# Two unread products around the products by lag, in rounds 3 to 7 of a state space layer on TensorE

## The reference

```python
def s5_mixer(h, w_in, a_re, a_im, log_dt, b_re, b_im, c_re, c_im, d_skip, w_glu, s_re, s_im):
    u = (h @ w_in).astype(f32).reshape(bsz, t, S5_GROUPS, S5_GROUP)
    ...
    bu_re = jnp.einsum('btgi,gpi->btgp', u, bb_re)
    bu_im = jnp.einsum('btgi,gpi->btgp', u, bb_im)
    ...
    _, _, x_re, x_im = lax.associative_scan(combine, (a_re_t, a_im_t, bu_re, bu_im), axis=1)
    y = (jnp.einsum('gip,btgp->btgi', c_re, x_re) - jnp.einsum('gip,btgp->btgi', c_im, x_im)
         + d_skip.astype(f32) * u).reshape(bsz, t, S5_WIDTH)
    za, zg = jnp.split(jax.nn.gelu(y).astype(h.dtype) @ w_glu, 2, axis=-1)
    return za * jax.nn.sigmoid(zg), x_re[:, -1], x_im[:, -1]
```

## Time and profile before

| | us |
|---|---|
| median of 3 runs | 1842.84 |
| lowest and highest run | 1841.28, 1846.24 |
| the profiled execution | 1847.72 |
| its span, first to last instruction | 1845.9 |
| TensorE busy, share of the span | 1734.2, 94% |
| VectorE, ScalarE, GpSimd busy | 1379.5, 1201.8, 146.4 |

### The profile page before, as it was taken

The page is one execution under the profiler, slowest core; times in us unless marked ns, Lnnn a source line. Parts: engine busy times, 40 slices in busy tenths (PEclk is TensorE's granted clock), DMA queues, the critical chain, the costliest instruction groups (busy, mean ns, idle before and its releaser), DMA issues.

```text
span 1845.9 us, 27103 instructions
## 1 busy us (share of the span) xinstructions
PE 1734.2 (94%) x9191; PEld 1457.0 (79%) x9191; DVE 1379.5 (75%) x1579; ACT 1201.8 (65%) x1491; POOL 146.4 (8%) x199
## 2 busy tenths in 40 slices
PE   6988899998899797999999999999999999999994
PEld 3877799986779695887887878878878788788884
DVE  3564445491643736998998989989989899899997
ACT  3623355303463445878888888888888888888885
POOL 1041000000044300700000000000000000000001
PEclk8988999999865698999999999999999999999997
DMA  8662654335630249998998989989989899899995
GB/s 349 257 258 90 237 194 160 141 151 194 289 137 1 103 178 382 399 418 323 422 367 348 410 312 419 392 325 420 360 358 400 314 422 380 343 412 355 399 376 197
DMA packets 72903, 553.49 MB, mean 300 GB/s; under 512 B 8256, under 2 KB 8527, under 8 KB 15328
## 3 DMA queue, kind: packets, MB, share of 16 engines
q1 hardware_dynamic: 69186, 538.54, 73.9%
q0 software_dynamic: 3072, 12.54, 1.8%
q10 hardware_dynamic: 542, 1.20, 0.2%
HBM read 530.74 MB, written 21.53 MB: 299 GB/s over the span
## 4 chain that ended last, share of the span: by engine, by line
PE 84%; DVE 6%; issue 4%; DMA 3%; ACT 2%; POOL 1%; ACTq 0%; DVEq 0%; POOLq 0%; SPq 0%
PE bank L1939 81%; PE bank L2406 1%; DMA ring<-in_dense_rows_dram 1%; DVE w_lo L516 1%; DMA arena<-in_state_conv_dram 1%; DVE arena L1686 1%; ACT w_hi L511 1%; DVE sq L1364 0%; PE bank L2385 0%; DVE rstd L1346 0%; ACT w_hi L463 0%; DVE w_lo L469 0%; DMA fT<-y_rows,row_i 0%; DVE sq L1517 0%; DVE arena L1899 0%
## 5 line engine op out<-in xcount | busy, mean ns | idle before, releaser
L1939 PE MATMUL bank<-w_hi,parts 128*128 128x512 f32 x3024 | 899.0, 392 | 14.8 <-DVE w_lo L516 13.3
L516 DVE TENSOR_TENSOR w_lo<-ring,w_hi 128x1024 fp32r<-128x1024 f32 x654 | 782.4, 1221 | 81.1 <-PE bank L1939 29.8
L511 ACT ACTIVATE w_hi<-ring 128x1024 fp32r<-128x1024 f32 x654 | 690.7, 1062 | 157.4 <-PE bank L1939 157.3
L1939 PEld LDWEIGHTS bank<-w_hi,parts 128*128 128x128 f32 x3024 | 561.6, 188 | 134.1 <-DVE w_lo L516 18.6
L1939 PE MATMUL bank<-w_lo,parts 128*128 128x512 f32 x1512 | 548.3, 390 | 0.0
L1939 PE MATMUL bank<-parts,w_hi 128*128 128x264 f32 x1600 | 312.6, 297 | 21.9 <-DVE parts L1353 21.9
L1939 PEld LDWEIGHTS bank<-w_lo,parts 128*128 128x128 f32 x1512 | 283.9, 188 | 60.3
L1939 PEld LDWEIGHTS bank<-parts,w_hi 128*128 128x128 f32 x1600 | 260.6, 198 | 33.9 <-issue 21.5
L1939 PE MATMUL bank<-parts,w_lo 128*128 128x264 f32 x800 | 234.0, 293 | 0.0
L469 DVE TENSOR_TENSOR w_lo<-ring,w_hi 128x2048 fp32r<-128x2048 f32 x50 | 114.5, 2295 | 148.2 <-ACT w_hi L463 148.2
L1939 PEld LDWEIGHTS bank<-parts,w_lo 128*128 128x128 f32 x800 | 158.0, 198 | 0.0
(11 more groups left out here) (412 smaller groups left out, 1289.4 us busy)
## 6 DMA issues: line engine op xcount, KB each, us to landing
ring<-in_expert_rows_dram SPq DMA_DIRECT2D x330, 1024.0 KB, 7.2
ring<-in_dense_rows_dram SPq DMA_DIRECT2D x48, 2048.0 KB, 8.3
hT<-in_expert_rows_dram SPq DMA_DIRECT2D x55, 1024.0 KB, 7.2
ring<-in_dense_rows_dram SPq DMA_DIRECT2D x8, 1408.0 KB, 6.4
x_rows<-arena SPq DMA_DIRECT2D x1, 7168.0 KB, 28.8
y_rows<-arena SPq DMA_DIRECT2D x10, 512.0 KB, 6.6
arena<-x_rows SPq DMA_DIRECT2D x9, 512.0 KB, 8.1
ring<-in_dense_rows_dram SPq DMA_DIRECT2D x2, 1024.0 KB, 4.8
```

The lines of the kernel that those rows point to most:

```text
L511: act.activation(hi_slots[u % AHEAD], raw_unit(u), ACT.Copy).then_inc(hi_ready, 1)
L516: dve.tensor_tensor(lo_slots[u % AHEAD], raw_unit(u), hi_slots[u % AHEAD].bitcast(F32), ALU.subtract).then_inc(lo_ready, 1)
L1939: return pe.matmul(out, lhsT, rhs, start=start, stop=stop, skip_group_check=True)
```

## The change

The outputs and lag products of a round get a product between them, and the lag products and chunk sums another. It multiplies the identity with the first 256 columns of `xT` and writes bank 0, where nothing reads it. The first stands in rounds 3 to 7, the second in rounds 3 to 6 (round 7 has no lag products): nine in all. Two waits come with it: for the writes of `xT` ahead of the first turns, and for ScalarE's copy of adaLN row 19 out of bank 0 ahead of the turns of tile 4, in round 3.

```diff
             def turns_of_b(k):
                 pe.wait_ge(b_pad_ready, k + 1)
                 if k:
                     pe.wait_ge(b_mat_ready, k)
+                if k == 4:
+                    pe.wait_ge(acc_free, TILE_AT[("ada", 19)] + 1)
                 for i in range(2):
...
+            def keep_busy():
+                pe.matmul(bank[0][:, 0:TP], ident[:, :], xT[:, 0, 0:TP], start=True, stop=True, skip_group_check=True)
...
             pe.wait_ge(c_now_ready, 1)
+            pe.wait_ge(x_ready, 2 * KT)
             pe.wait_ge(acc_free, TILES["in1"] + KT)
...
                 if k >= 2:
                     outputs(k - 2)
+                if 3 <= k < KT:
+                    keep_busy()
                 if k + 1 < KT:
                     lag_products(k + 1)
+                    if k >= 3:
+                        keep_busy()
                     chunk_sums(k + 1)
```

## The result

The changed kernel takes 1852.57 us (median of 19 runs) where the kernel before, run beside it, takes 1843.94 (19 runs). The ratio is 1.0045 with a 95% interval of 1.0033 to 1.0057: 8.3 us slower, with 6.1 to 10.5. The forecast was 1847.8, or 5.0 us more. The direction was right, the size was not, and the time lies above the range of 1841.0 to 1851.5. Of the 4.8 us above the forecast 1.1 are the kernel before itself, whose median was 1842.84 when the forecast was made.

What follows compares the result with a forecast made beforehand. The bound was the state space layer's chain of outputs, lag products and 6.08 us of other engines, at half clock. Fillers 4.5 plus row 19 wait 0.5 made 5.0 us on the median 1842.84: 1847.8, range 1841.0 to 1851.5.

Steps and rivals of the forecast that it cites:

- The path: State space layer, rounds 4 to 6: outputs, lag products, then 6.08 us of other engines before the next outputs; period 14.61 us.
- The fillers' price: Each added product in rounds 3 to 7 costs 0.85 us at half clock, 0.43 at full clock; all nine priced at half.
- their sum: Nine fillers on the path: 1.70 us in round 3, 0.99 each in rounds 4 and 5, 0.85 in round 6.
- The term of 4.5 us: Rounds 3 to 7: the fillers' whole cost, 4.53 us, with nothing behind the rounds giving it back.
- rival B: Rounds 3 to 6: the filler ahead tips the clock up for the lag products in some rounds; 1842 us, chance 17%.
- The two waits: Ahead of the first turns, the xT wait costs nothing; ahead of round 3's turns, the row 19 wait costs 0.5 us.
- rival C: Round 3: the pause before the turns keeps the clock down, outputs lose 2.1 us; 1849.4 to 1851.1 us, chance 22%.
- That premise: Whole trace: stretches where the clock steps are not tied to the program, so other executions are hit elsewhere or not at all.
- rival A: Rounds 3 to 7: the fillers hold the clock up, a round takes 10.9 us instead of 14.61; 1826.7 us, chance 8%.
- One reading of the prediction against rival A: Before 637.3 us: the clock fell in TensorE's wait of 4.3 us, taken as evidence that idle time lowers it.

Runs made afterwards that it cites:

- the version with products in the wait alone: Six unread products ahead of the outputs of rounds 3 to 8, none beside the lag products, against the kernel before: 0.9979, 1840.3 us.
- the version with the wait filled: Changed kernel plus six unread products between turns and outputs in rounds 3 to 8: 0.9942 of the kernel before, 1834.4 us; without the xT wait 0.9928, 1830.0 us.

## Why the prediction was right and wrong

**The path was right.** Lag products, then 6.08 us of the other engines, then outputs: behind the lag products of rounds 4 to 6 it holds in every trace (6.1 us) but that of the version with products in the wait alone. The fillers of the changed kernel are in the places foreseen, in round 7 within the wait (4.27 us left of 5.22).

**The fillers' price was about right, their sum was not.** Fillers with the wait for xT against that wait alone, start of the outputs counted from the first turns: round 4 is 1.75 us later, round 5 2.60, round 6 3.44. The sum had 1.70, 2.69, 3.68. But then the rounds part. In the timeline of the fillers without the wait for row 19, round 6:

```profile
595.89 0.67 PE L1939 MATMUL bank<-arena,plain_lo 128*128 128x72 f32 x2
596.36 0.75 PE L1939 MATMUL bank<-plain_parts,plain_hi 128*128 128x72 f32 x4
596.95 0.39 PE L1939 MATMUL bank<-arena,plain_lo 128*128 128x72 f32 x2
...
598.96 0.64 PE L2251 MATMUL bank<-xT,ident 128*128 128x256 f32 x2
599.44 1.85 PE L1939 MATMUL bank<-arena,plain_hi 128*128 128x16 f32 x16
```

The clock rises in the outputs, and the rest of the outputs and the lag products take half as long: at the glu product 0.04 us is left of 3.44. **The term of 4.5 us was in fact 0.0 net** in the changed kernel's course, with the wait for row 19 as without it, and 3.4 where the wait for xT is out too. In the same trace TensorE was busy all the time at half clock until the rise:

```profile
552.50:596.00 43.50, 43.50 (x194) 0.50 0.03 14
```

All six traces with fillers at the sides alone have such a rise (in round 4, 5 or 6), of the nine without fillers four have one, in round 4, where no pause stands ahead of the outputs either. This is rival B by another door: the rise comes in the outputs, ahead of the filler, and in five of the six in a round where the filler behind the lag products had closed the pause of 0.71 us ahead of the outputs. In the first trace of the changed kernel it comes in round 4, where no such pause stands in any version without fillers. So the closed pause may be the cause in five and isn't in the sixth; no run isolates it, and why the clock rises just there stays open.

**The two waits are the steps that failed.** The wait for xT was put at nothing, and cost 3.7 us in the stretch (221.2 to 224.9). It waits for nothing; issuing it takes 0.15 us, and this moves the kernel from its common course to the other. I could not see this in one trace: the execution of the earlier trace rows was by chance already in the other course. It was there to be read that it stood 4.9 us above its median, and I set the sum on the median but the mechanism on the trace.

The wait for row 19 was put at 0.5 us, and cost 3.0 beside the wait for xT. I saw what it could do (rival C's 2.1 us for the outputs), but gave it a quarter, since I held that the clock's steps were not tied to the program. **That premise was wrong.** In all 18 traces the rise ahead of the layer stands 22.6 to 23.0 us before the first turns, and the next fall 4.3 to 4.6 us or 8.1 to 8.2 us behind them. So what one execution shows at half a microsecond's distance from a step is no lottery; it comes back in nearly every execution. That the rise stands ahead of round 3's outputs only in some executions was true of the kernel before, where one trace of five has it there. But the wait for xT puts the changed kernel into just that course, and without that wait the one for row 19 costs nothing in the trace.

I also counted only the outputs. Their 2.1 us is what the rounds show: the adaLN product behind them begins 2.05 us later with the wait than without it (118.19 against 116.14 us behind the first turns, both without fillers). Of these 1.0 comes back by the glu product, which the prediction had ruled out, and 2.0 is lost in the glu stage, where the clock comes up 5.5 us behind the first product instead of 3.2. Rival C comes nearest, but its 6.6 to 8.3 us rest on 4.5 for the fillers, which the runs don't bear out.

The whole, from the stretches and added in this order: 3.7 for the wait for xT, 3.0 for the wait for row 19, 0.0 net for the fillers: 6.7 us, with 8.3 (6.1 to 10.5) and 7.0 (3.9 to 10.3) measured. The forecast had 0, 0.5 and 4.5. That it came within 3.3 us of the difference measured, and on the right side, is luck: it has 6.2 us too little for the waits and 4.5 too much for the fillers.

The Trainium skill's rule of rival A ("TensorE: Matmul & The Clock Gate", Part 1: activity releases the throttle) was right in direction, and the version with the wait filled shows what it gives here: 10.7 us with the waits, 13.3 without the one for xT. But activity alone didn't bring the clock up soon: TensorE was busy for 43.5 us on end at half clock before the rise above. The same part of the Trainium skill's page says that what watches the activity runs freely and doesn't start anew with the kernel; here the clock's rise kept its distance from the first turns to 0.5 us in all traces. Why it does is not shown. One reading of the prediction against rival A was wrong too: the clock did not fall while TensorE waited 4.3 us before 637.3. The earlier trace rows has a grant of 1.00 over that wait, and the fall comes at its end.

## What to carry to other kernels

Where TensorE's clock moves up and down, compare a stretch over several executions before a change is costed on it: two courses of the same kernel can differ by more than the change. Here unread products paid where they filled the waits (3.9 us), and most with some on the sides of the narrow products too (10.7 us); on the sides alone they gained nothing. A wait that is already satisfied is not free ahead of a place where the clock decides: leave it out where another wait implies it. One that isn't satisfied yet cost nothing where the engine waited anyway (the wait for row 19, ahead of the outputs). Price two small edits together and not each alone, when both stand near such a place: here one decided what the other cost.

## What the runs showed of the hardware

- One more satisfied wait ahead of TensorE's first turns: 0.15 us (0.53 to 0.68), with either of the two semaphores tried.
- For the same instructions two courses of the clock: 131.2 or 125.0 us from the first turns to the glu product. Which one follows went by 0.15 us of idle time in 17 of 18 traces, and by the distance to the rise ahead (up to 22.66 us, or 22.70 and more) in all 18.
- TensorE can be busy for 43.50 of 43.50 us, with narrow f32 products and turns, at a grant of 0.50.
- At full clock a plain f32 product of 256 columns takes 0.43 us among its like (twelve records in 2.76 us, the last one's own 0.38 taken off), as foreseen, and 0.48 to 0.52 between other products; at half clock 0.95 to 1.0 there (0.85 foreseen).
